# Dense expert gates written by accumulating indirect DMAs into a zeroed DRAM matrix, in place of one-hot products

## The reference

```
q = (h @ w_q)                                  # 8 heads x 2 halves of 128
v1, i1 = top_k(q1 . keys_a, 16); v2, i2 = top_k(q2 . keys_b, 16)
top_s, pos = top_k(v1[:,None] + v2[None,:], 16)
idx = i1*128 + i2 at pos;  gates = softmax(top_s)      # 8 x 16 experts for each token
act = gelu(h . expert_u[idx])
y   = sum over the 128 picks of gates * act * expert_v[idx]
```

## Time and profile before

| | |
|---|---|
| median of 3 runs (lowest to highest) | 1668.12 us (1666.88 to 1669.82) |
| span of the profiled execution | 1668.3 us |
| TensorE busy | 1590.2 us, 95% |
| VectorE busy | 1281.9 us, 77% |
| ScalarE, POOL busy | 722.5 us, 422.3 us |
| DMA | 426.84 MB, mean 256 GB/s |

### The profile page before, as it was taken

One profiled execution on the slowest core, in us unless ns is written; L12 is line 12 of the kernel. 1 busy time (PEld: TensorE's weight loads), 2 busy tenths in 40 slices (PEclk: granted clock), 3 DMA queues, 4 the chain that ended last, 5 costly groups with the idle time before them and its releaser, 6 DMA issues.

```text
span 1668.3 us, 23725 instructions
## 1 busy us (share of the span) xinstructions
PE 1590.2 (95%) x8101; PEld 1388.0 (83%) x8101; DVE 1281.9 (77%) x2618; ACT 722.5 (43%) x1188; POOL 422.3 (25%) x390
## 2 busy tenths in 40 slices
PE   5899899897899999999999999999999999999996
PEld 3787655676899999999999999998888888888885
DVE  6665333736858999999999999936888888888888
ACT  4223375326334343434367776734333333333333
POOL 0000133132423332332312222201333333333330
PEclk8999899998999999999999999999999999999998
DMA  8573300003668878878979899879999999999992
GB/s 319 211 286 119 126 1 1 1 26 136 222 214 270 276 235 287 288 246 257 322 235 324 303 330 316 320 271 314 339 352 359 350 356 351 362 350 358 350 354 98
DMA packets 176964, 426.84 MB, mean 256 GB/s; under 512 B 15168, under 2 KB 99280, under 8 KB 172112
## 3 DMA queue, kind: packets, MB, share of 16 engines
q1 hardware_dynamic: 139984, 291.14, 49.8%
q0 software_dynamic: 36864, 134.23, 23.3%
HBM read 372.88 MB, written 52.43 MB: 255 GB/s over the span
## 4 chain that ended last, share of the span: by engine, by line
PE 71%; DVE 1%; issue 0%; ACT 0%; DVEq 0%; ACTq 0%
PE ps_y L1874 10%; PE ps_y L1878 10%; PE ps_y L1876 10%; PE ps_u L1091 10%; PE ps_u L1092 10%; PE ps_u L1093 10%; PE ps_g L1586 5%; PE ps_q L1273 1%; PE ps_q L1275 1%; PE ps_q L1274 1%; PE ps_s L1285 1%; DVE y_scaled L1849 0%; DVE row L1856 0%; PE ps_u L1898 0%; DVE y_row L1170 0%
## 5 line engine op out<-in xcount | busy, mean ns | idle before, releaser
L1091 PE MATMUL ps_u<-h_hi,u_hi 128*128 128x384 f32 x1024 | 349.4, 341 | 1.7 <-DVE u_lo L1081 1.7
L1093 PE MATMUL ps_u<-h_hi,u_lo 128*128 128x384 f32 x1024 | 345.1, 337 | 0.0
L1092 PE MATMUL ps_u<-h_lo,u_hi 128*128 128x384 f32 x1024 | 345.0, 337 | 0.0
L1150 POOL DMA_INDIRECT row<-in_v,row_index x128 | 176.4, 1378 | 401.9 <-DVE y_row L1170 306.3
L1753 ACT CAST v_hi<-v_raw 128x1024 fp32r<-128x1024 f32 x128 | 134.7, 1053 | 327.4 <-issue 327.4
L1150 POOL DMA_INDIRECT row<-in_u_rows,row_index x128 | 151.1, 1181 | 451.1 <-DVE row_dots L1157 381.5
L1810 DVE TENSOR_TENSOR v_lo<-v_raw,v_hi 128x1024 fp32r<-128x1024 f32 x128 | 160.7, 1255 | 103.1 <-ACT v_hi L1753 103.1
L1874 PE MATMUL ps_y<-v_hi,w_hi 128*128 128x512 f32 x768 | 237.5, 390 | 0.0
L1878 PE MATMUL ps_y<-v_hi,w_lo 128*128 128x512 f32 x768 | 236.5, 389 | 0.0
L1876 PE MATMUL ps_y<-v_lo,w_hi 128*128 128x512 f32 x768 | 236.5, 389 | 0.0
L1081 DVE TENSOR_TENSOR u_lo<-u_raw,u_hi 128x1024 fp32r<-128x1024 f32 x128 | 166.9, 1310 | 79.7 <-ACT u_hi L1074 79.6
(11 more groups left out here) (275 smaller groups left out, 2369.1 us busy)
## 6 DMA issues: line engine op xcount, KB each, us to landing
u_raw<-in_u SPq DMA_DIRECT2D x128, 512.0 KB, 5.0
v_raw<-in_v SPq DMA_DIRECT2D x128, 512.0 KB, 6.2
w_ada<-in_w_ada SPq DMA_DIRECT2D x24, 1024.0 KB, 6.6
activations<-u_act SPq DMA_DIRECT2D x128, 192.0 KB, 5.2
gate_tiles<-g_tile SPq DMA_DIRECT2D x12, 2048.0 KB, 9.2
gates<-gate_tiles SPq DMA_DIRECT2D x32, 768.0 KB, 9.0
act<-activations SPq DMA_DIRECT2D x128, 192.0 KB, 6.4
w_proj<-in_w_proj SPq DMA_DIRECT2D x16, 512.0 KB, 4.0
```

The source lines that it names most:

```text
L1091: pe.matmul(out, self.hi[n][:, k], hi, start=(k == 0), stop=False)
L1092: pe.matmul(out, self.hi[n][:, k], lo, start=False, stop=False)
L1093: last = pe.matmul(out, self.lo[n][:, k], hi, start=False, stop=(k == KD - 1))
L1150: pool.indirect_dma_start(out=self.row[n][:], out_offset=None, in_=self.table[q // PICKS], in_offset=bass.IndirectOffsetOnAxis(ap=self.ind ...
```

## The change

1. `dense_gates` goes, with its transposes, one-hot tiles, `ps_g` matmuls, copies and stores, and so does the constant `iota`. In its place `up_only` holds U blocks 80 to 119 with dots 81 to 127 and nothing else.
2. The gates live in one DRAM matrix of 16384 x 384 fp32 (25.2 MB), one 4-byte element a row. SP writes zeros to all of it in `stick_breaking` (32 DMAs of 786 KB from a zeroed tile) and waits there until they have landed.
3. For each head, dense tile of 128 tokens and pick, POOL issues one indirect DMA that adds 128 gates (one a partition, 4 bytes) to their places: 8 x 3 x 16 = 384 scatters. VectorE works out the places. `gather_and_scatter` puts them ahead of the gathers: 36 in each of the turns 2 to 7, 168 in `up_only`.
4. The low parts of query weights (14 operations of 128 x 1024) move from POOL to VectorE.
5. In `experts`, SP waits for all scatters ahead of the fourth-last U block's end, and loads one gate tile of 192 KB for each V block. V-row additions begin at U block 122 (seven blocks earlier) and end at V block 121.

```diff
+SCATTERED_BY = [0, 0, 0, 36, 72, 108, 144, 180, 216]
+ZEROED = 16 * (N_KEYS * DENSE // ZERO)
...
@@ stick_breaking, SP @@
+            sp.wait_ge(zeros_made, 1)
+            for n in range(N_KEYS * DENSE // ZERO):
+                sp.dma_start(g_dram[n * P * ZERO:(n + 1) * P * ZERO].rearrange("(p z) o -> p (z o)", p=P), zero[:])\
+                  .then_inc(g_zeroed, 16)
+            sp.wait_ge(g_zeroed, ZEROED)
...
@@ stick_breaking, POOL @@
+            pool.memset(zero[:], 0.0).then_inc(zeros_made, 1)
...
@@ PickedRows @@
+    def scatter(self, pool, s, g_dram, g_zeroed):
+        h, b, k = s // (DENSE_TILES * TOPK), s // TOPK % DENSE_TILES, s % TOPK
+        j = h * TOPK + k
+        if s == 0:
+            pool.wait_ge(g_zeroed, ZEROED)
+        pool.wait_ge(self.placed, h + 1)
+        pool.wait_ge(self.gated, h + 1)
+        if h > 0 and k == 0:
+            pool.wait_ge(self.scattered[b], 16 * TOPK * h)
+        pool.indirect_dma_start(out=g_dram, out_offset=bass.IndirectOffsetOnAxis(ap=self.place[:, b, j:j + 1], axis=0),
+                                in_=self.gate[:, 1 + b, j:j + 1], in_offset=None, compute_op=ALU.add)\
+            .then_inc(self.scattered[b], 16)
...
@@ retrieval, POOL @@
-                if h < LAST:
-                    pool.wait_ge(s_copied, 2 * h + 2)
-                    query_low(h + 1)
-                for r in range(gathered(h), gathered(h + 1)):
-                    rows.gather(pool, r)
+                gather_and_scatter(pool, rows, g_dram, g_zeroed, range(gathered(h), gathered(h + 1)),
+                                   range(SCATTERED_BY[h], SCATTERED_BY[h + 1]))
...
@@ retrieval, VectorE @@
+                if h == 0:
+                    query_low(1)
...
+                if h + 2 <= LAST:
+                    query_low(h + 2)
...
-                note(dve.tensor_copy(expert[:, :, h * TOPK:(h + 1) * TOPK], picked[:]))
+                dve.scalar_tensor_tensor(rows.place[:, :, h * TOPK:(h + 1) * TOPK], picked[:, 1:TB], float(DENSE),
+                                         rows.base[:].broadcast_to([P, DENSE_TILES, TOPK]), ALU.mult, ALU.add).then_inc(rows.placed, 1)
...
+def gather_and_scatter(pool, rows, g_dram, g_zeroed, gathers, scatters):
+    n = max(1, len(gathers))
+    for q in range(n):
+        for s in scatters[q * len(scatters) // n:(q + 1) * len(scatters) // n]:
+            rows.scatter(pool, s, g_dram, g_zeroed)
+        for r in gathers[q:q + 1]:
+            rows.gather(pool, r)
...
@@ up_only @@
+    def vector(dve):
+        for b in range(FIRST, TAIL_U):
+            up.vector_at(dve, b)
+            for r in dots_at(b):
+                rows.dot(dve, r, h_row)
+    def tensor(pe):
+        for b in range(FIRST, TAIL_U):
+            up.product(pe, b)
...
@@ experts @@
-        FIRST_ADD = 1
+        FIRST_ADD = 2 - OPENING
...
+                if i == 5 - OPENING:
+                    for b in range(DENSE_TILES):
+                        sp.wait_ge(rows.scattered[b], 16 * PICKS)
+                    for n in range(3):
+                        load_gates(n)
```

More of the change, by code:

```diff
@@ L52 @@
 DENSE_TILES = DENSE // P
-G_TOK = 32
-G_TILES = DENSE // G_TOK
+SCATTERS = DENSE_TILES * PICKS
 ROW_READS = 2 * PICKS
@@ L1142, in __init__ @@
         self.row_used, self.indexed, self.acted, self.weighed = sem("row_used"), sem("row_indexed"), sem("row_gelu"), sem("row_weighed")
+        self.placed, self.gated, self.based = sem("gates_placed"), sem("gates_made"), sem("token_place_made")
+        self.scattered = [sem(f"gates_scattered{b}") for b in range(DENSE_TILES)]
     def gather(self, pool, q):
@@ L1170, in add, with retrieval @@
             dve.scalar_tensor_tensor(y, self.row[n][:], col, y, ALU.mult, ALU.add).then_inc(self.row_used, 1)
-def retrieval(nc, life, io, keep, picks, up, rows, h_row, query):
+def retrieval(nc, life, io, keep, up, rows, h_row, query, g_dram, g_zeroed):
     with ExitStack() as ctx:
@@ L1354, in vector, with query_low @@
             dve.wait_ge(iota_done, sum(r for _, r, _, _ in PAIR_PARTS))
+            def query_low(h):
+                for s in range(2):
+                    dve.wait_ge(wq_hi, h * 2 + s + 1)
+                    dve.wait_ge(q_done, h * 2 + s - 1)
+                    dve.tensor_tensor(w_lo[s][:], w[s][:], w_hi[s][:].bitcast(F32), ALU.subtract).then_inc(wq_lo, 1)
             def turn(h):
@@ L1648, in experts @@
+def experts(nc, life, io, keep, up, rows, h_row, g_dram):
     with ExitStack() as ctx:
@@ L1660, in experts @@
         w_lo = [sb(f"w_lo{n}", [P, DENSE], F32R) for n in range(WS)]
-        gates = [sb(f"gates{n}", [P, G_TILES, QUAD, G_TOK]) for n in range(2)]
+        gates = [sb(f"gates{n}", [P, DENSE]) for n in range(GS)]
         flat = lambda t: t[:].rearrange("p k e -> p (k e)")
@@ L1672, in experts @@
         a_in = [sem(f"a_in{n}") for n in range(AS)]
-        g_in = [sem(f"g_in{n}") for n in range(2)]
+        g_in = [sem(f"g_in{n}") for n in range(GS)]
         fin_in, stored = sem("g_final_in"), sem("stored")
@@ L1814, in vector @@
                     up.vector_at(dve, N_KEYS + i)
-                if i == -2:
+                if i == 1 - OPENING:
                     dve.wait_ge(rows.acted, 1)
-                    dve.tensor_tensor(rows.weight[:], rows.weight[:], rows.gate[:], ALU.mult).then_inc(rows.weighed, 1)
+                    dve.tensor_tensor(rows.weight[:], rows.weight[:], rows.gate[:, 0], ALU.mult).then_inc(rows.weighed, 1)
                 if block_ok(i + 1):
@@ L1899, in turned @@
                 last.then_inc(extra, 1)
-            for b in range(GATED, N_KEYS):
+            for b in range(TAIL_U, N_KEYS):
                 up.product(pe, b)
@@ L1945, in program @@
         acts = nc.dram_tensor("activations", [N_KEYS, P, DENSE], F32, kind="Internal").ap()
-        g_stored = [top.enter_context(nc.semaphore(f"g_stored{n}")) for n in range(2)]
         up = UpProducts(nc, top, io, keep, acts)
         rows = PickedRows(nc, top, io)
-        with ExitStack() as front:
-            fsb = lambda n, s, d=F32: front.enter_context(nc.sbuf_tensor(n, s, d))
-            picks = (fsb("expert", [P, TB, P]), fsb("gate", [P, TB, P]))
-            h_row = fsb("h_row", [P, D])
-            first = retrieval(nc, top, io, keep, picks, up, rows, h_row, query)
-            query_banks.close()
-            second = dense_gates(nc, top, keep, picks, up, rows, h_row, g_dram, g_stored)
-        third = experts(nc, top, io, keep, up, rows, g_dram, g_stored)
+        h_row = sb("h_row", [P, D])
+        first = retrieval(nc, top, io, keep, up, rows, h_row, query, g_dram, g_zeroed)
+        query_banks.close()
+        second = up_only(up, rows, h_row, g_dram, g_zeroed)
+        third = experts(nc, top, io, keep, up, rows, h_row, g_dram)
         block = top.enter_context(nc.Block())
```

259 lines of the change are left out of this document (61 added, 198 removed).

## The result

| | before | after |
|---|---|---|
| median (lowest to highest) | 1668.53 us (1666.88 to 1669.82) | 2028.07 us (2023.26 to 2029.52) |
| span of the profiled execution | 1668.3 us | 2021.2 us |
| first product of the V blocks | 1126.8 us | 1478.1 us |

The ratio is 1.2146, with a 95% interval of 1.2127 to 1.2165: 21% slower. That is 264 us over the forecast of 1764 us (257 us by the span) and above the upper end of the range, 1900 us. The direction came as forecast, and so did the mechanism; the price of one scatter did not.

The account below looks back on a forecast made before the run. TensorE bounds the kernel before; POOL's indirect DMAs were to bound the changed one. V-stage start 517 + 504 x 1.40 = 1223 us, plus 541 us to the end, gives 1764 us; range 1565 to 1900 us.

Parts of the forecast that it names:

- What bounds the kernel, and the direction: TensorE bounds the kernel before; POOL, with most room, gets 384 more instructions and sets the pace: slower, chance 0.45.
- Every sign listed for this case: In `retrieval` and `up_only`: POOL busy or in 0.30 us gaps, VectorE awaiting rows, TensorE awaiting u_lo over 150 us.
- c: POOL's mean time per indirect DMA, over 504 until the last gate: 1.40 us taken, upper bound 1.85, break-even 1.21.
- The price moves with VectorE: Stretched turns hold fewer VectorE operations a microsecond, so 1.40 us was taken per POOL DMA instead of 1.44.
- The prediction's rule: On POOL, a gather issued during a VectorE operation with two SBUF operands waits for its end, then 0.90 us more.
- Rival A: Scatters under 1.15 us on POOL with gap, TensorE stays the bound: down to 1569 us, chance 0.33.
- Rival B: Additions choke the DMA engines, up to 2094 us, or scatters are dearer on POOL too: over 1915 us, chance 0.17.
- the crossover of 0.67 us: Time a scatter holds the 16 DMA engines at which their bound, 449 + 384d, overtakes POOL's 706 us.
- TensorE's gain of 94 us: Between turn 7 and the V stage, one-hot products, nine transposes and the wait ahead of them go: 94 us.
- The low parts of query weights, 5 us gained: VectorE makes them in time, ending TensorE's 4.3 us wait, with half a microsecond of lowered clock: 5 us gained.
- Zeroing, hidden: 25.2 MB of zeros take 73 us inside SP's idle 91.1 us, costing 0; other bound 19 us.
- The end: From the V stage's start to the end: 542.1 us before, 1 us less for earlier V-row additions, bounds 0 and 3.7.

Follow-up runs that it names:

- Kernel 1: The changed kernel with no scatter issued and no wait for them, dense gates left out: 1586.36 us, ratio 0.9497 to the kernel before.
- kernel 3: The changed kernel with all 384 scatters writing their gates plainly instead of adding them: 1834.47 us.
- kernel 2: The changed kernel with half of the scatters, 192, the other half of the dense gates left out: 1676.36 us, ratio 1.0044 to the kernel before.
- kernel 7: The changed kernel without scatters, dense gates left out, and with head 2's low part at the end of turn 0: 1578.17 us, ratio 0.9455.
- kernel 6: The kernel before with low parts of query weights made by VectorE, head 2's at the end of turn 0: 1666.90 us, ratio 0.9986.
- kernel 5: The kernel before with only the low parts of query weights moved to VectorE, at the changed kernel's places: 1673.41 us, ratio 1.0028.
- kernel 8: The kernel before with kernel 6's query weights and one of three dense tiles moved from one-hot products to 128 scatters: 1668.54 us, ratio 1.0002.

## Why the prediction was right or wrong

**What bounds the kernel, and the direction.** Right: POOL had the most room and got more than it could hold, and TensorE waits through gather, dot and `u_lo`. Kernel 1 shows it: without the scatters TensorE is busy throughout. Every sign listed for this case is there: gaps of 0.30 us, 468 us of VectorE waiting for rows, 284 us of TensorE waiting for `u_lo` (over 150 us was asked), the longest `u_lo` down from 3.47 us to 1.30 us.

**The term that failed is c, the mean time of POOL for one indirect DMA.** I took 1.40 us from the gathers, with 1.85 us as the upper bound; it was (1469 - 512) / 504 = 1.90 us. What stands ahead of these DMAs and behind them was nearly as taken. Counted as the prediction counts, with the first extra of the V stage as its start (1476 us here), it is 512 + 957 + 7 + 545 = 2021 us against 502 + 706 + 15 + 541 = 1764 us. Of the 257 us between, 251 are c, 10 the late start, 4 the end, and 8 are given back, as 7 us and not 15 lie between the last scatter and the V stage. The error was that of the nearest row. A scatter without the addition is indeed priced as a gather: 0.98 us against 0.94 us. The addition puts 0.60 us on it, 384 x 0.60 = 230 us here, and kernel 3 is 194 us faster for its absence (the rest went back into longer DMAs beside a denser VectorE, 1.324 us a gather against 1.217). By kernel 3 without additions c was (1280 - 514) / 504 = 1.52 us, inside my bounds. The bound above was wrong in kind, too: it was the dearest run of gathers, which says nothing of what another operation costs. I had put a dearer scatter, "a target read for each piece", under the second rival with over 1915 us. That is the case that came, and it had belonged in the forecast's bounds, since the text itself saw no reason to exclude it.

**The price moves with VectorE.** Right in sign, and too small in size: I wrote that stretched turns hold fewer VectorE operations a microsecond. They do, and the scatter falls from 1.79 to 1.66 us; but the same relation makes the price rise as soon as the loss is mended, 2.01 us in the turns of kernel 2. For this reason kernel 2 took 1676 us and not the 1638 us of constant prices. The prediction's rule, that a gather issued beside an operation with two SBUF operands waits for its end, holds for DMAs that begin while the operation runs, and not for one that has begun ahead of it (kernel 2). Its 0.90 us behind the end is 0.82 us by the records: hot_j ends at 896.58 + 1.22 = 897.80 us and the gather at 898.62 us. No term of the sum hangs on that.

The Trainium skill, SBUF — State Buffer, "Who interferes with whom", infers that a tensor_tensor doesn't hold up descriptor generation. The traces speak against the inference: `u_lo` is a tensor_tensor, and the 12 scatters that began inside one, with no other long VectorE operation beside them, all end 1.43 to 1.45 us behind it.

**Rival A, scatters cheap.** Out: the shortest scatter takes 1.55 us, where this rival needed 1.15 us with its gap. Its 1569 us for an unloaded POOL was near: kernel 7 takes 1578 us, with a span of 1576.8 us. Where the 8 us between them lie is told under TensorE's gain.

**Rival B, the DMA engines.** Out as the bound: the share fell to 0.62 to 0.71, and POOL hardly waited ahead of a scatter for anything but the 0.30 us gaps (116.8 of 117.1 us), so never for an earlier one to land. The time that a scatter holds the 16 engines is d = (27.6% x 2021.2 - 23.3% x 1668.3) / 384 = (557.8 - 388.7) / 384 = 0.44 us, under the crossover of 0.67 us. Kernel 2 says the same: 1804 us would have been due. This rival's last group, a scatter dearer on POOL too and a time over 1915 us, is what came, on POOL alone.

The Trainium skill, DMA: Bandwidth & Descriptors, "Measured", has 0.68 us for a 4 KB transfer of 128 rows; the 0.44 us of a scatter with addition lies below it.

**TensorE's gain of 94 us.** Right within 10%: kernel 7 starts the V blocks 1121.5 - 1035.7 = 85.8 us earlier than kernel 6, from which it differs by the rest of the change without its scatters. The first matmul of the last U block in turn 7, in kernel 6 and in kernel 7, and its last matmul in the kernel before:

```profile
826.09 0.34 PE L1091 MATMUL ps_u<-h_hi,u_hi 128*128 128x384 f32 x1
```
```profile
831.09 0.34 PE L1099 MATMUL ps_u<-h_hi,u_hi 128*128 128x384 f32 x1
```
```profile
835.34 0.34 PE L1093 MATMUL ps_u<-h_hi,u_lo 128*128 128x384 f32 x1
```

Kernel 7 is 5.0 us late already there; why, no run shows. And 831.94 us was misread: it is a row of ScalarE in the chain, while TensorE works at the last block of turn 7 until 835.7 us. So 290.5 us and not 294.2 lie behind it, and less the 200 us of U blocks 90.5 us were to be gained and not 94.

**The low parts of query weights, 5 us gained.** Wrong in sign as the change does it (kernel 5: 0.28% slower) and right in size if the pair of turn 0 is placed behind its input (kernel 6 by its span; by the medians it is 2 us). The half microsecond of lowered clock was too little: from 450 to 505 us the mean granted clock was 0.94 in the kernel before and 1.00 in kernel 6, 55 x 0.06 = 3.3 us. I priced the subtractions' 14 x 1.2 us and didn't ask whether ScalarE has made the input by then; in the changed kernel it delays POOL's start, part of the 10 us above.

**Zeroing, hidden.** Right. SP still waits 20.3 us for the stage's end of its former 91.1 us, so the zeros took 71 us where I took 73 us, 25.2 MB at 355 GB/s. **The end.** 545 us in the changed kernel and 541.9 us in kernel 7, where I took 541 us: the one microsecond for the V-row additions can't be told from this.

## What to carry to other kernels

An indirect DMA with an addition is not priced by an indirect DMA without one: where the trace of before has no row for an operation, its upper bound is a reason, not the dearest row of another operation. When work goes to an engine with room, count instructions times their mean with the gap against the time that the engine has, stage by stage: POOL was busy 25% of the span before, and yet 504 instructions of 1.9 us make 957 us where breaking even left no more than 625 us (502 to 1127 us). The mean isn't fixed: it is taken from rows with the load of VectorE that the new kernel will have. And when a step is moved to another engine, look where its input is made and when, before its cost is counted.

## What the runs showed of the hardware

- An indirect DMA that adds 128 elements of 4 bytes to DRAM takes POOL 1.55 us at least and 1.58 us in the median, one that only writes or reads them 0.94 to 0.98 us; 0.30 us pass between two.
- It makes 144 packets, as a gather of 128 rows of 4 KB does, and 32 without the addition. The engines are held 0.44 us by it, against 1.52 us by such a gather (23.3% x 1668.3 / 256).
- It is lengthened where it begins inside a long operation of VectorE: behind a `u_lo` it ends 1.43 to 1.45 us after it (12 of 12); one that begins ahead of `u_lo` isn't held up (22 of 22 took at most 1.65 us). So its mean grows with VectorE's share of the stretch: 1.66, 1.72, 1.79 us at 25%, 48% and 65%, and 2.01 us at 89% (kernel 2).
- The same decides over the gathers of V rows, which take 1.79 us in the mean in kernel 8 and 1.38 us in kernel 6, though no scatter is left when they run. Kernel 6, POOL and VectorE:

```profile
1299.13 1.92 POOL L1150 DMA_INDIRECT row<-in_v,row_index  x1 [3.21 <-DVE y_row L1170]
1303.14 0.94 POOL L1150 DMA_INDIRECT row<-in_v,row_index  x1 [2.08 <-DVE y_row L1170]
```
```profile
1299.02 1.23 DVE L1813 TENSOR_TENSOR v_lo<-v_raw,v_hi 128x1024 fp32r<-128x1024 f32 x1 [0.65 <-ACT v_hi L1756]
1303.10 1.29 DVE L1813 TENSOR_TENSOR v_lo<-v_raw,v_hi 128x1024 fp32r<-128x1024 f32 x1 [0.72 <-ACT v_hi L1756]
```

  A gather that begins 0.11 us behind the start of `v_lo` takes 1.93 us, one that begins 0.04 us behind it 0.94 us. In kernel 6 the two alternate; in kernel 8 106 of 128 begin 0.10 or 0.11 us behind. Why 0.04 us is not enough to be held up, no run shows.
